# Swiglu by seven half products: eighteen per FFN instead of eleven, with h kept in DRAM meanwhile

## What is computed

```python
def _swiglu(x, w_gate, w_up, w_down):
    hid = jax.nn.silu(jnp.einsum('bsd,df->bsf', x, w_gate)) * jnp.einsum('bsd,df->bsf', x, w_up)
    return jnp.einsum('bsf,fd->bsd', hid, w_down)
for l in range(DEPTH):
    h = h + 0.5 * _swiglu(_rmsnorm(h, ffn1_norm[l]), ffn1_w_gate[l], ffn1_w_up[l], ffn1_w_down[l])
    h = h + _hybrid_mixer(_rmsnorm(h, mix_norm[l]), ...)
    h = h + 0.5 * _swiglu(_rmsnorm(h, ffn2_norm[l]), ffn2_w_gate[l], ffn2_w_up[l], ffn2_w_down[l])
```

## Time and profile before

| | before |
|---|---|
| median of 3 runs | 3229.08 us (3227.15 to 3229.86) |
| the profiled execution's own time | 3232.4 us |
| span of its trace | 3230.5 us |
| mean granted TensorE clock | 0.992 |
| TensorE busy | 3167.1 us |
| VectorE busy | 2025.7 us |
| ScalarE busy | 1457.1 us |
| POOL busy | 71.0 us |
| read from HBM | 291.03 MB |

### The profile page before, as it was taken

One profiled execution on the slowest core, in us unless ns is written; L12 is line 12 of the kernel. 1 busy time (PEld: TensorE's weight loads), 2 busy tenths in 40 slices (PEclk: granted clock), 3 DMA queues, 4 the chain that ended last, 5 costly groups with the idle time before them and its releaser, 6 DMA issues.

```text
span 3230.5 us, 43458 instructions
## 1 busy us (share of the span) xinstructions
PE 3167.1 (98%) x17020; PEld 2697.5 (83%) x17020; DVE 2025.7 (63%) x3095; ACT 1457.1 (45%) x2145; POOL 71.0 (2%) x137
## 2 busy tenths in 40 slices
PE   9999999999999999999999999999999999999998
PEld 7988876788988899887678898888888888889987
DVE  7853565767843686346575785467766687468633
ACT  5542335454532454233545553346445476345422
POOL 0000000100000000000010000000000000000000
PEclk9999999999999999999999999999999999999999
DMA  4333322122333233332211233332322223323331
GB/s 142 105 110 95 97 82 75 34 69 85 102 113 99 87 98 117 95 97 88 69 46 43 92 105 115 97 104 92 105 92 82 87 91 102 106 85 99 118 91 66
DMA packets 102746, 296.80 MB, mean 92 GB/s; under 512 B 15440, under 2 KB 26464, under 8 KB 102544
## 3 DMA queue, kind: packets, MB, share of 16 engines
q1 hardware_dynamic: 96336, 277.91, 27.2%
q0 software_dynamic: 5344, 14.02, 1.6%
q10 hardware_dynamic: 864, 2.10, 0.2%
HBM read 291.03 MB, written 2.95 MB: 91 GB/s over the span
## 4 chain that ended last, share of the span: by engine, by line
PE 85%; DVE 7%; ACT 5%; issue 2%; DMA 1%; POOL 0%; DVEq 0%; ACTq 0%; POOLq 0%
PE ps L928 26%; PE ps L930 26%; PE ps L929 26%; PE ps L937 2%; ACT wh L1579 1%; DVE wl L2226 1%; DVE mf L2539 1%; ACT L1559 1%; PE ps L942 1%; PE ps L1460 1%; PE ps L1307 1%; PE ps L1340 1%; PE ps L1456 0%; PE ps L1390 0%; ACT mf L2140 0%
## 5 line engine op out<-in xcount | busy, mean ns | idle before, releaser
L1579 ACT ACTIVATE wh<-raw 128x1024 fp32r<-128x1024 f32 (+3 forms) x634 | 621.9, 982 | 1105.6 <-PE ps L930 1063.2
L2226 DVE TENSOR_TENSOR wl<-raw,wh 128x1024 fp32r<-128x1024 f32 (+3 forms) x634 | 716.0, 1129 | 512.2 <-ACT wh L1579 508.8
L928 PE MATMUL ps<-hnh,wh 128*128 128x512 f32 (+1 forms) x2492 | 918.8, 369 | 6.9 <-DVE hnl L2345 3.3
L929 PE MATMUL ps<-hnl,wh 128*128 128x512 f32 (+1 forms) x2492 | 904.5, 363 | 0.0
L930 PE MATMUL ps<-hnh,wl 128*128 128x512 f32 (+1 forms) x2492 | 904.3, 363 | 0.0
L928 PE MATMUL ps<-mr,wh 128*128 128x512 f32 (+1 forms) x2180 | 758.4, 348 | 0.9 <-DVE mr L2844 0.5
L930 PE MATMUL ps<-mr,wl 128*128 128x512 f32 (+1 forms) x2180 | 755.3, 346 | 0.0
L929 PE MATMUL ps<-mr,wh 128*128 128x512 f32 (+1 forms) x2180 | 754.9, 346 | 0.0
L928 PEld LDWEIGHTS ps<-hnh,wh 128*128 128x128 f32 x2492 | 473.7, 190 | 86.4 <-issue 11.4
L930 PEld LDWEIGHTS ps<-hnh,wl 128*128 128x128 f32 x2492 | 473.2, 190 | 74.0
L929 PEld LDWEIGHTS ps<-hnl,wh 128*128 128x128 f32 x2492 | 473.9, 190 | 71.8 <-issue 2.7
(11 more groups left out here) (343 smaller groups left out, 2826.4 us busy)
## 6 DMA issues: line engine op xcount, KB each, us to landing
raw<-in_w_in SPq DMA_DIRECT2D x140, 512.0 KB, 3.4
raw<-in_ffn_w_gate SPq DMA_DIRECT2D x87, 512.0 KB, 3.5
raw<-in_ffn_w_up SPq DMA_DIRECT2D x87, 512.0 KB, 4.2
raw<-in_ffn_w_down SPq DMA_DIRECT2D x64, 512.0 KB, 3.5
raw<-in_w_ffn_in SPq DMA_DIRECT2D x44, 512.0 KB, 3.5
raw<-in_ffn_w_down SPq DMA_DIRECT2D x32, 384.0 KB, 3.1
raw<-in_w_out SPq DMA_DIRECT2D x32, 256.0 KB, 2.7
mf<-cs_rows POOLq DMA_DIRECT2D x32, 256.0 KB, 3.8
```

What stands on the lines that cost most here:

```text
L928: self.e.matmul(out, ah, bh, start=start, stop=False, skip_group_check=shared)
L929: self.e.matmul(out, ah, bl, start=False, stop=False, skip_group_check=shared)
L1579: self.e.activation(k.spl[k.spl_of[u]][0][:, 0:n], x[:, 0:n], ACT.Copy).then_inc(k.w_hi, 1)
L2226: self.e.tensor_tensor(lo[:, 0:n], x[:, 0:n], hi[:, 0:n].bitcast(F), ALU.subtract).then_inc(k.w_lo, 1)
```

## The change

All pairs from 2 to 10 go by sevens, gate and up. The token-side sums then live until the end of the run, past the writing of `hid` tiles 14 to 19, so they move: `turned(0)` stays in slots 40 to 43, `turned(1)` and `turned(2)` take the place of h itself, and `turned(3)` that of the second token halves of `hn` tiles 0 to 3, which no product reads any more once the plain products are done. POOL stores h to DRAM (2 MB) when ScalarE has read it, and loads it back when the last seven's "c1" is done (`swap_h`). ScalarE's h3 and h2, which overwrite h, wait for the store; VectorE's `add_h` waits for the load.

The steps change too. ScalarE now multiplies h by the gain's column, 16 copies of 128 x 256 in two steps ("x1", "x2"), and VectorE adds and subtracts four tiles at once, 128 x 1024. Before, VectorE did both, four instructions of 256 columns for each of six sums. The last sum is split in a step 9 of its own, after A1 of the first seven. `F_PACE` goes from 0.6 to 0.7. Sizes, weights, loads and results are the same.

```diff
--- before.py
+++ after.py
@@ -76,11 +76,11 @@
 S_W, S_S, S_LO, S_DD, S_EC, S_SQ = (33, 34, 35, 8), 36, 37, 41, 43, 44
 L_Y, L_U, L_YL, L_UH, L_R, L_I = (17, 21, 25, 37, 13), (29, 31), (33, 35), 9, 41, 43
 OUT_T, H_ROWS, LAST_H = 100, 44, 44
-F_T, F_D, F_X, F_3, F_2, F_4, F_PACE = (28, 32, 36, 40), 12, 14, 16, 18, 20, 0.6
+F_1, F_D, F_X, F_3, F_2, F_4, F_PACE = 40, 12, 14, 16, 18, 20, 0.7
 F_GAIN = (("ffn1_norm", 0), ("ffn2_norm", 0), ("ffn1_norm", 8), ("ffn2_norm", 8), ("norm2_w_2", 0))
 
 
-SEVEN = {p: (up,) for p, up in ((2, True), (3, True), (4, False), (5, True), (6, True), (7, True))}
+SEVEN = {p: (True,) for p in range(2, 11)}
 PLAIN, OF_3, OF_24, OF_1 = range(4)
 A1, E3, B2, A12, C1, B22, C4 = range(7)
 L_GATE, L_HI, L_LO = (35, 36), (9, 10, 11, 12, 41, 42, 43, 44), (29, 30, 31, 32, 33, 34, 35, 36)
@@ -174,7 +174,7 @@
         self.ffn_s, self.ffn_a, self.ffn_v, self.ffn_h = (steps(n, x) for n, x in (("ffn_s", "silu"), ("ffn_a", "hi"), ("ffn_v", "lo"), ("ffn_h", "rs")))
         self.add_v, self.se_p = steps("add_v", "s3 s1 s2 s4"), steps("se_p", "a1 b2 c1")
         self.se_a, self.se_v = steps("se_a", "b c e s"), steps("se_v", "c22 c21 c2 c1")
-        self.ft_v, self.ft_a = steps("ft_v", "d x t3 t2 l1 t4 l3 l2 l4"), steps("ft_a", "h1 h3 h2 h4")
+        self.ft_v, self.ft_a = steps("ft_v", "t1 t3 t2 t4 l1 l3 l2 l4"), steps("ft_a", "x1 x2 h1 h3 h2 h4")
 
         self.sp_a, self.sp_v = steps("sp_a", "abs exp ln inv"), steps("sp_v", "u m ratio rest out")
         self.zeroed, self.row_a, self.row_v = sem("zeroed"), sem("row_hi"), sem("row_lo")
@@ -243,7 +243,12 @@
             self.at += -(-width * 4 // 64) * 64
             return t
 
-        self.h = [place(f"h{i}", T) for i in range(8)]
+        self.h_base = self.at
+        self.h_all = place("h", 8 * T)
+        self.h = [self.h_all[:, T * i:T * i + T] for i in range(8)]
+        self.h_sums = [nc.alloc_sbuf_tensor_at(f"hs{i}", [128, 1024], R, offset=self.h_base + 4096 * i) for i in range(4)]
+        self.h_save = nc.dram_tensor("h_save", (128, 8 * T), F).ap()
+        self.h_out, self.h_back = sem("h_out"), sem("h_back")
         self.hn_base = self.at
         self.hn = [(place(f"hnh{i}", T, R), place(f"hnl{i}", T, R)) for i in range(8)]
         self.raw = [place(f"raw{i}", 1024) for i in range(NRAW)]
@@ -291,7 +296,13 @@
         return self.raw[r % NRAW], self.raw_in[r % NRAW], 16 * (r // NRAW + 1)
 
     def turned(self, n):
-        return self.slot(F_T[n], 2, R), self.slot(F_T[n] + 2, 2, R)
+        return (self.slot(F_1, 2, R), self.slot(F_1 + 2, 2, R)) if n == 0 else self.h_sums[2 * n - 2:2 * n]
+
+    def moving(self, n, j):
+
+        if n == 3:
+            return [x[:, 256:512] for x in self.hn[j]]
+        return [x[:, 256 * j:256 * j + 256] for x in self.turned(n)]
 
     def part(self, i, h):
 
@@ -572,6 +583,8 @@
             self.between(n, a, i, hid)
             if n == A1:
                 self.end_pair()
+                if i == 2 * min(SEVEN) and not hid:
+                    self.halves_step(f, 9)
             if n in (E3, A12, B22, C4):
                 if n == A12:
                     self.made()
@@ -1042,8 +1055,8 @@
                 hi, lo = k.hn[j if n == A1 else j + 4]
                 s = slice(256, 512) if n == C4 else slice(0, 256)
             else:
-                hi, lo = k.turned(moving)
-                s = slice(256 * j, 256 * j + 256)
+                hi, lo = k.moving(moving, j)
+                s = slice(0, 256)
             up = None
             if j == 3:
                 up = k.se_p.up(w, {A1: "a1", B2: "b2", C1: "c1"}[n])[0] if n in (A1, B2, C1) else k.unit_done
@@ -1618,16 +1631,28 @@
     def halves_step(self, f, n):
         k, e = self.k, self.e
         gain, g = F_GAIN[f]
-        if n == 1:
-            self.wait_ge(*k.ft_v.at(f, "d"))
+        if n in (0, 1):
+            self.wait_ge(k.h_set, 8)
+            for x, half, first in (((F_2, 0, 0), (F_X, 256, 0)), ((F_3, 256, 4), (F_4, 0, 4)))[n]:
+                for j in range(4):
+                    m = e.activation(k.slot(x, 2)[:, 256 * j:256 * j + 256], k.h[first + j][:, half:half + 256], ACT.Copy,
+                                     scale=k.cl(gain, g + first + j))
+            m.then_inc(*k.ft_a.up(f, f"x{n + 1}"))
+        elif n == 3:
+            self.wait_ge(*k.ft_v.at(f, "t1"))
+            e.activation(k.turned(0)[0][:, :], k.slot(F_D, 2)[:, :], ACT.Copy).then_inc(*k.ft_a.up(f, "h1"))
+        elif n in (6, 7):
+            name, at, x, scale = (("3", 1, F_3, 1.0), ("2", 2, F_2, -1.0))[n - 6]
+            self.wait_ge(*k.ft_v.at(f, "t3" if n == 6 else "t2"))
+            self.wait_ge(*k.ft_a.at(f, "x2"))
+            self.wait_ge(k.h_out, 16 * (f + 1))
+            e.activation(k.turned(at)[0][:, :], k.slot(x, 2)[:, :], ACT.Copy, scale=scale).then_inc(*k.ft_a.up(f, "h" + name))
+        elif n == 9:
+            self.wait_ge(k.unit_done, self.u)
+            self.wait_ge(*k.ft_v.at(f, "t4"))
             for j in range(4):
-                s = slice(256 * j, 256 * j + 256)
-                m = e.activation(k.turned(0)[0][:, s], k.slot(F_D, 2)[:, s], ACT.Copy, scale=k.cl(gain, g + j))
-            m.then_inc(*k.ft_a.up(f, "h1"))
-        elif n in (3, 5, 6):
-            name, at, x, scale = {3: ("3", 1, F_3, 1.0), 5: ("2", 2, F_2, -1.0), 6: ("4", 3, F_4, -1.0)}[n]
-            self.wait_ge(*k.ft_v.at(f, "t" + name))
-            e.activation(k.turned(at)[0][:, :], k.slot(x, 2)[:, :], ACT.Copy, scale=scale).then_inc(*k.ft_a.up(f, "h" + name))
+                m = e.activation(k.moving(3, j)[0], k.slot(F_4, 2)[:, 256 * j:256 * j + 256], ACT.Copy, scale=-1.0)
+            m.then_inc(*k.ft_a.up(f, "h4"))
 
     def ffn_silu(self, f, i):
         k = self.k
@@ -2283,51 +2308,36 @@
 
     def halves_step(self, f, n):
         k, e = self.k, self.e
-        gain, g = F_GAIN[f]
-        one, two = slice(0, 256), slice(256, 512)
         at = [slice(256 * j, 256 * j + 256) for j in range(4)]
         d, x, t3, t2, t4 = (k.slot(i, 2) for i in (F_D, F_X, F_3, F_2, F_4))
-        col = lambda j: k.cl(gain, g + j)
-        if n == 0:
-            self.wait_ge(k.h_set, 8)
-            for j in range(4):
-                m = e.tensor_tensor(d[:, at[j]], k.h[j][:, one], k.h[j][:, two], ALU.subtract)
-            m.then_inc(*k.ft_v.up(f, "d"))
-        elif n == 1:
-            for j in range(4):
-                m = e.tensor_scalar(x[:, at[j]], k.h[j][:, two], col(j), None, ALU.mult)
-            m.then_inc(*k.ft_v.up(f, "x"))
-        elif n == 2:
-            self.wait_ge(*k.ft_v.at(f, "x"))
-            for j in range(4):
-                m = e.scalar_tensor_tensor(out=t3[:, at[j]], in0=k.h[j + 4][:, two], scalar=col(j + 4), in1=x[:, at[j]],
-                                           op0=ALU.mult, op1=ALU.subtract)
-            m.then_inc(*k.ft_v.up(f, "t3"))
+        if n == 2:
+            self.wait_ge(*k.ft_a.at(f, "x1"))
+            e.tensor_tensor(d[:, :], t2[:, :], x[:, :], ALU.subtract).then_inc(*k.ft_v.up(f, "t1"))
         elif n == 3:
+            self.wait_ge(*k.ft_a.at(f, "x2"))
+            e.tensor_tensor(t3[:, :], t3[:, :], x[:, :], ALU.subtract).then_inc(*k.ft_v.up(f, "t3"))
+        elif n == 4:
             self.wait_ge(*k.ft_v.at(f, "t3"))
-            for j in range(4):
-                m = e.scalar_tensor_tensor(out=t2[:, at[j]], in0=k.h[j][:, one], scalar=col(j), in1=t3[:, at[j]],
-                                           op0=ALU.mult, op1=ALU.add)
-            m.then_inc(*k.ft_v.up(f, "t2"))
-        elif n == 4:
-            self.wait_ge(*k.ft_a.at(f, "h1"))
-            hi, lo = k.turned(0)
-            for j in range(4):
-                m = e.scalar_tensor_tensor(out=lo[:, at[j]], in0=d[:, at[j]], scalar=col(j), in1=hi[:, at[j]].bitcast(F),
-                                           op0=ALU.mult, op1=ALU.subtract)
-            m.then_inc(*k.ft_v.up(f, "l1"))
+            e.tensor_tensor(t2[:, :], t2[:, :], t3[:, :], ALU.add).then_inc(*k.ft_v.up(f, "t2"))
         elif n == 5:
             self.wait_ge(*k.ft_v.at(f, "t2"))
-            for j in range(4):
-                m = e.scalar_tensor_tensor(out=t4[:, at[j]], in0=k.h[j + 4][:, one], scalar=col(j + 4), in1=t2[:, at[j]],
-                                           op0=ALU.mult, op1=ALU.subtract)
-            m.then_inc(*k.ft_v.up(f, "t4"))
-        else:
-            name, to, t, scale = (("3", 1, t3, 1.0), ("2", 2, t2, -1.0), ("4", 3, t4, -1.0))[n - 6]
+            e.tensor_tensor(t4[:, :], t4[:, :], t2[:, :], ALU.subtract).then_inc(*k.ft_v.up(f, "t4"))
+            hi, lo = k.turned(0)
+            self.wait_ge(*k.ft_a.at(f, "h1"))
+            e.tensor_tensor(lo[:, :], d[:, :], hi[:, :].bitcast(F), ALU.subtract).then_inc(*k.ft_v.up(f, "l1"))
+        elif n in (7, 8):
+            name, to, t, scale = (("3", 1, t3, 1.0), ("2", 2, t2, -1.0))[n - 7]
             hi, lo = k.turned(to)
             self.wait_ge(*k.ft_a.at(f, "h" + name))
```

(20 more changed lines are left out.)

## The result

The changed kernel takes 3207.31 us (median of 4 runs, 3206.73 to 3208.36); the kernel before, beside it, 3228.8. The profiled execution lasted 3206.73 us, its span is 3204.9: 25.6 less than the span of before, whose profiled execution, of 3232.4 us, lay 3.3 above the median of 3229.08.

The account below looks back on a forecast made before the run. TensorE, busy 98% of the span, was taken to bound the kernel. Terms of -28.0 (more sevens), +6.0 (end wait) and +8.9 (gate 1 waits) made -13.1 us, from the median 3229.08 to 3216.0; range 3205 to 3228.

Parts of the forecast that it names:

- The run of sevens: In each FFN, 18 products by sevens instead of 11, at 10.08 us each: 28.0 us saved over five FFNs.
- rival (d): VectorE becomes the bound of the sevens; at 10.25 us a product the gain would be gone, 3231 us; chance 0.07.
- The wait at the end: Before each FFN's first down product, TensorE waits 1.2 us for VectorE's c1; five times, +6.0 us.
- The waits for gate 1's take: In FFNs 2 to 5, TensorE waits about 1.1, 3.4, 3.4 and 2.2 us for VectorE; +8.9 us over today.
- Rival (a): The plain products don't wait, as ScalarE's copies find room before the split; -22.0 us, 3207 us; chance 0.17.
- The clock: TensorE's clock after waits in the FFNs; the sum counted no fall to 1.2 GHz.
- rival (b): The clock falls after TensorE's long waits; two falls cost 3.4 to 6.8 us, 3219 to 3223 us; chance 0.18.
- my two waits of 3.4 us: TensorE's forecast waits for gate 1's take in the third and fourth FFN, 3.4 us each.
- h to DRAM: POOL's 2 MB store and load of h in each FFN, 8.3 to 10 us per transfer, costing nothing.
- rival (c): The store of h lands late, at 17.2 us, holding h3, l3 and up 1's take; 3235.6 us; chance 0.08.
- The step that failed: In the two mixers, interleaved steps shift by 0.4 and 0.2 of a step; taken as 0, 2 us either way each.

Follow-up runs that it names:

- the kernel of the four steps: Changed kernel with ScalarE's 16 copies in four steps of four instead of two of eight, h1 and l1 before the second eight: 3192.7 us, ratio 0.9893.
- first run: Changed kernel with the step counter entering both mixers at the old remainders (0.40, 0.40 instead of 0.80, 0.20): 3218.49 us, ratio 0.997.
- second run: Kernel before with the step counter entering the mixers at the changed kernel's remainders (0.80, 0.20), nothing else changed: 3213.43 us, ratio 0.9956.
- the kernel with both waits out: Changed kernel without `banks_back` at the end of the sevens and with ScalarE's 16 copies in four steps of four: 3186.79 us, ratio 0.9865.

## Why the prediction was right, and where it was not

**The run of sevens** was right: 18 products at 10.08 us, VectorE at 18.71 of 20.16, so rival (d) fell, and the 28.0 us came (187.09 less 181.44 is 5.65 for an FFN, 28.2 in all). The 120 ns of the earlier trace rows held. The Trainium skill (TensorE: Matmul & The Clock Gate, "Back-to-back issue gap") gives 262 cycles, or 109 ns, for isolated matmuls of 256 columns, by which the forecast's estimate was 41.7; the trace differs, and the measurement decides.

**The wait at the end** was right in its chain and size: 1.17 us against 1.2, 5.85 in all; taking it out gave 4.9 us on the changed kernel and 5.9 on the one with four steps.

**The waits for gate 1's take** were right in place and size: 1.0, 3.4, 3.4 and 2.1 us against 1.1, 3.4, 3.4 and 2.2, in sum 8.6 against 8.9. The timeline shows the chain of the forecast, and the kernel of the four steps shows that the waits hang on the steps ahead of the take. It does not part the chain's two links, the block of copies ahead of the split and the four whole-tile instructions behind it, since it moves both. Rival (a) is wrong, though its number, 3207, is the one measured.

**The clock** was decided wrongly for the sum, which had no fall; two falls came, as in rival (b), for the least that it reckoned with, 3.4 us, but only one in a place that it named. Which places could not be told from the length: the clock fell in the third and the fifth FFN, at waits of 3.4 and 2.1 us, in the fourth not at one of 3.4, and in the run without the bank wait it did there too. The forecast reckoned with falls behind "my two waits of 3.4 us" alone. The Trainium skill (TensorE: Matmul & The Clock Gate, Part 1) has the gate closed by default and opened by activity; two of these three waits agree, and none of these rows shows why the third does not.

**h to DRAM** cost nothing, as forecast: the store took 6.5 to 8.8 us where 8.3 to 10 were reckoned, the load 9.1 to 10.6, and rival (c), at 17.2, was far off. That nobody waits is read from the rows; a kernel without the swap wasn't tried.

**The step that failed** is a term of the sum: "The new remainders also shift the two mixers' interleaved steps by 0.4 and 0.2 of a step: I take 0 and keep 2 us either way for each." They are worth 11.2 us on the changed kernel (first run) and 14.7 on the kernel before (second run), a gain, and some three times the 4 us that the two bounds make together. A shift of under one step was taken for small; but steps go whole, one by one, at given places of strict queues, and a shift by less than a step can put one instruction ahead of a split that waits for ScalarE or behind it, with 1.5 to 5 us of TensorE at stake each time, and the clock behind it. With the old remainders the changed kernel takes 3218.49 us, 2.5 above the forecast, and there the clock's 3.4 is what the sum lacked; that 3207.31 lies in the range too is not the sum's merit. That the term was a gain is luck of these values: on the kernel with both waits out, 0.60 costs 9.4 us against 0.80 and 0.20, and 0.00 costs 12.1.

**The sum again**, in the sizes measured: -28.2 + 5.85 + 8.6 + 3.4 = -10.35 for the FFNs, where the run with the old remainders gives 9.7, and 11.2 for the mixers: -21.55, and -21.5 was measured. That it closes so well is partly chance, since the runs can be taken the other way round: the new remainders on the kernel before give 14.7, which leaves 6.1 (3213.43 less 3207.31) for the edits to the FFNs. The traces lay that difference to the clock, with 13.7 us at half clock in the two mixers' stretches of the kernel before with new remainders and 20.5 in those of the changed kernel, which makes 3.4. In the profiled spans the mixers gave 8.56 + 0.4 and 2.50 + 2.8 us, when the waits of the FFNs inside those stretches are taken out, 14.2; with the FFNs' 10.35 and the start's 1.9 that makes 26.4, where the spans differ by 25.6. The other 0.9 us lie in the three stretches without a mixer or sevens, which are 0.2 to 0.5 us longer than wait and clock explain.

What stays open is why the clock falls behind one wait and not behind another of the same length, and with it a few us in any of these kernels: in a mixer's stretch the half clock ranges from 3.4 to 20.5 us.

## What to carry to other kernels

When work is interleaved by a counter, its remainder is a parameter of every later stage: changing a pace in one stage shifts whole steps in the next, and no product there need change for two stages to move by 16 us together. Before crediting a change with its time, compare stage by stage, and run the old kernel with the new phase and the new with the old. A block of copies on one engine ahead of a split that a second engine waits for can become a wait on a third: spread such steps so that what the third engine needs stands ahead of them, with the work the same.

## What was not expected of the hardware

The clock fell to 1.2 GHz for 3.4 us after a wait of TensorE of 2.1 us, and stayed at 2.4 GHz after one of 3.4 us, in one execution of the changed kernel. And on one queue, POOL's, the 2 MB store to DRAM landed in 6.6 us (median of five), while the load of the same bytes took 9.7.
